# A hybrid attention layer on one core: transposes of keys, queries and augmented rows become float32r products with a float32r identity

## The reference

```python
def dsa_mixer(q, k, v, iq, iw, ik):                       # 8 heads, one shared key/value head
    logits = einsum('bqhd,bsd->bqhs', iqb, ik)             # indexer, 8 heads of 32
    index = einsum('bqh,bqhs->bqs', iwb, relu(logits)) * idx_scale
    _, sel = top_k(index, 256)                            # keys kept for each query
    s = einsum('bqhd,bqkd->bqhk', qb, kg) * scale
    return einsum('bqhk,bqkd->bqhd', masked_softmax(s, valid), vg)

def nsa_mixer(q, k_cmp, v_cmp, k_slc, v_slc, k_win, v_win, gates, ...):   # 8 heads in 2 groups
    kc, vc = compress(k_cmp), compress(v_cmp)             # 127 compressed keys
    # compressed branch, 8 selected blocks of 64 keys, and a window of 512 keys
    return gb[..., 0:1] * o_c + gb[..., 1:2] * o_s + gb[..., 2:3] * o_w
```

## Time and profile before

| | |
|---|---|
| median of three executions | 4019.19 us (4006.82 to 4023.22) |
| the profiled execution, its own time | 4008.02 us |
| its span, first to last instruction | 4006.0 us |
| PE busy over the span | 3669.9 us, 92% |
| DVE, ACT, POOL busy | 46%, 41%, 19% |
| granted clock, mean | 0.945 |

### The profile page before, as it was taken

How to read it: one execution, slowest core, us unless ns; L and a number is a source line. 1 busy time by engine, 2 the same in 40 slices (tenths; PEclk the granted TensorE clock), 3 DMA queues, 4 the chain that set the end, 5 groups by cost and what they waited for, 6 DMA issues and landing times. The chain is left out here.

```text
span 4006.0 us, 56003 instructions
## 1 busy us (share of the span) xinstructions
PE 3669.9 (92%) x19448; PEld 3110.9 (78%) x19448; DVE 1838.5 (46%) x4296; ACT 1650.0 (41%) x2690; POOL 765.1 (19%) x1650
## 2 busy tenths in 40 slices
PE   6999768989898999999999697999999999999997
PEld 5999647877777788888778585788788788878885
DVE  4222145666666666776664343333343243324323
ACT  2000024667666677677765332232232233223321
POOL 0000023454343333332321132000020020002001
PEclk9999768999999999999889898999999999999998
DMA  4221220000000000000000354333333433433342
GB/s 144 74 69 62 67 50 26 24 16 22 16 9 16 15 16 13 10 7 10 4 6 6 124 158 147 105 94 129 103 94 112 135 100 94 142 109 96 94 136 74
DMA packets 302064, 273.15 MB, mean 68 GB/s; under 512 B 32544, under 2 KB 249760, under 8 KB 299680
## 3 DMA queue, kind: packets, MB, share of 16 engines
q1 hardware_dynamic: 300368, 268.31, 21.8%
q10 hardware_dynamic: 1488, 2.20, 0.2%
HBM read 218.57 MB, written 51.90 MB: 68 GB/s over the span
## 5 line engine op out<-in xcount | busy, mean ns | idle before, releaser
L2224 DVE TENSOR_TENSOR f_w_lo<-f_raw,f_w_hi 128x1024 fp32r<-128x1024 f32 x264 | 337.3, 1278 | 883.7 <-ACT f_w_hi L2176 883.7
L2176 ACT ACTIVATE f_w_hi<-f_raw 128x1024 fp32r<-128x1024 f32 x264 | 279.9, 1060 | 882.6 <-PE f_acc L2128 337.2
L1285 ACT ACTIVATE a_p_t<-a_ps_st 128x512 f32<-128x512 f32 x716 | 438.0, 614 | 371.3 <-PE a_ps_st L1175 191.7
L1292 ACT ACTIVATE a_junk_a<-a_index,a_tk 128x384 bf16<-128x384 f32 (+13 forms) x336 | 445.0, 1325 | 110.3 <-DVE a_halves L1402 55.6
L1201 PEld LDWEIGHTS a_ps_o<-a_vsl,a_p_t 128*128 128x128 f32 x2176 | 315.5, 209 | 26.4 <-DVE a_fin L1499 3.4
L2128 PE MATMUL f_gate<-f_x_hi,f_w_hi 128*128 128x512 f32 x704 | 275.1, 391 | 30.2 <-DVE f_w_lo L2224 30.2
L1201 PE MATMUL a_ps_o<-a_vsl,a_p_t 128*128 128x65 f32 x2176 | 298.2, 284 | 2.1 <-DVE a_fin L1499 2.1
L1201 PEld LDWEIGHTS a_ps_o<-a_dv,a_p_t 128*128 128x128 f32 x2176 | 290.0, 194 | 9.0
L2128 PE MATMUL f_acc<-f_w_hi,f_g_hi 128*128 128x512 f32 x704 | 278.6, 396 | 16.4 <-DVE f_y L2280 12.6
L2128 PE MATMUL f_acc<-f_w_lo,f_g_hi 128*128 128x512 f32 x704 | 277.2, 394 | 0.0
L2128 PE MATMUL f_acc<-f_w_hi,f_g_lo 128*128 128x512 f32 x704 | 277.0, 393 | 0.0
(11 more groups left out here) (268 smaller groups left out, 7556.7 us busy)
## 6 DMA issues: line engine op xcount, KB each, us to landing
f_raw<-in_w_gate SPq DMA_DIRECT2D x88, 512.0 KB, 3.8
f_raw<-in_w_up SPq DMA_DIRECT2D x88, 512.0 KB, 3.8
f_raw<-in_w_down SPq DMA_DIRECT2D x88, 512.0 KB, 3.3
z_scratch<-p_z SPq DMA_DIRECT2D x16, 1120.0 KB, 5.2
pw_raw<-in_w_in SPq DMA_DIRECT2D x16, 560.0 KB, 3.8
px_raw<-in_x_t SPq DMA_DIRECT2D x16, 512.0 KB, 6.4
o_scratch<-a_oacc SPq DMA_DIRECT2D x32, 256.0 KB, 2.1
m_o_in<-o_scratch SPq DMA_DIRECT2D x16, 512.0 KB, 4.5
```

What stands on the lines that cost most here:

```text
L1285: act.activation(p_t[:, s % PT_RING, :], ps_st[s % ST_BANKS][:, :], ACT.Exp, scale=SCALE).then_inc(exp_done, 1)
L1292: act.activation(junk_a[:, 0:w], index[t % 2][:, 0:w], ACT.Sign, bias=thr, scale=-1.0, accum_out=cnt).then_inc(counted, 1)
L2176: act.activation(w_hi[:, slot], raw[:, parity], ACT.Copy).then_inc(hi_done, 1)
L2224: dve.tensor_tensor(w_lo[:, slot], raw[:, parity], w_hi[:, slot].bitcast(F32), ALU.subtract).then_inc(lo_done, 1)
```

## The change

Each transposed block becomes an ordinary product of the block, as float32r, with a float32r copy of the identity. The shapes, the operands' roles, the number of TensorE instructions and their order stay: the stationary operand is the block, the moving operand the identity. VectorE makes the copy `ident_r` once, ahead of its other set-up, and TensorE's first transposes wait for that copy instead of for the constants. The augmented rows are declared float32r, so that the three instructions that write them write float32r. The transposes of the compression and mixing stages are not touched.

```diff
+        ident_r = sb("a_ident_r", [P, P], F32R)
...
-        aug_n = sb("a_naug", [P, 2, 8, P])
-        aug_d = sb("a_daug", [P, 8, P])
+        aug_n = sb("a_naug", [P, 2, 8, P], F32R)
+        aug_d = sb("a_daug", [P, 8, P], F32R)
...
-            pool.memset(aug_n[:, :, :, :], 0.0).then_inc(aug_clear, 1)
-            pool.memset(aug_d[:, :, :], 0.0).then_inc(aug_clear, 1)
+            pool.memset(aug_n[:, :, :, :].bitcast(F32), 0.0).then_inc(aug_clear, 1)
+            pool.memset(aug_d[:, :, :].bitcast(F32), 0.0).then_inc(aug_clear, 1)
...
                     src = split[:, b, :] if kind in "KI" else q_hi[:, b].rearrange("p a d -> p (a d)")
-                    mm = pe.transpose(out[:, (b - b0) * P:(b - b0 + 1) * P], src.bitcast(F32), const("ident", 0, P))
+                    mm = pe.matmul(out[:, (b - b0) * P:(b - b0 + 1) * P], src, ident_r[:, :], start=(b == b0), stop=(b == b0 + nb - 1), skip_group_check=True)
                 mm.then_inc(group_turned, 1)
...
-                    mm = pe.transpose(out[:, h * P:(h + 1) * P], aug_of(kind, i)[:, 4 * g + h, :], const("ident", 0, P))
+                    mm = pe.matmul(out[:, h * P:(h + 1) * P], aug_of(kind, i)[:, 4 * g + h, :], ident_r[:, :], start=(h == 0), stop=(h == 3), skip_group_check=True)
                 mm.then_inc(group_turned, 1)
...
-            pe.wait_ge(const_ld, 32)
+            pe.wait_ge(ident_set, 1)
...
             dve.wait_ge(const_ld, 32)
+            dve.tensor_copy(ident_r[:, :], const("ident", 0, P)).then_inc(ident_set, 1)
             mine(dve.tensor_copy(ident_b[:, :], const("ident", 0, P)))
```

More of the change, by code:

```diff
@@ L783, in attention_phase @@
         rows_set = sem("a_rows_set")
+        ident_set = sem("a_ident_set")
         split_done = {k: sem(f"a_split{k}") for k in "KIND"}
```

## The result

The changed kernel takes 4077.36 us, the median of six runs (4065.42 to 4088.94), and the kernel before takes 4013.64 us over its six (4005.95 to 4023.22). The ratio is 1.0157, with a 95% interval of 1.0132 to 1.0181, so the change costs 64 us. The forecast was 4080. The two profiled executions lie a little further apart than the medians, 72 us (4080.2 and 4008.0).

What follows compares the result with a forecast made beforehand. TensorE was taken to bound the attention stage, busy 91% at a mean clock of 0.92. Direct price +10 and clock +54 make +64 us on the profiled 4008.0, or 4072; with the median's offset 4080, range 4030 to 4120.

Steps and rivals of the forecast that it cites:

- TensorE sets the pace and is priced twice, by stream and by clock: Attention stage: TensorE busy 91%; a product costs what it takes from the stream and what it does to the clock.
- The direct price: TensorE's 976 blocks: +0.003 us each and an exposed load behind each of 158 runs, +10 us in all.
- Later rises: Attention stage: blocks stream half as long, so 22 clock rises come later, 154 us more at low clock, 64 us lost.
- The 7 us for each rise: Delay assumed for each of 22 rises, from nine low stretches that ended without transposes, 7.2 us in the mean.
- the one row of 17.0 us: Low stretch from 1919.3 to 1936.3 without a transpose at its end, TensorE busy for 16.65 us; the longest of nine.
- A sixth of it lost in waits: Attention stage: a slower TensorE finds VectorE's maxima ready, so the clock's 64 us become 54 us.
- The number of low stretches about as now: Profile after, attention stage: about as many stretches at clock 0.50 as the 31 before, each longer.
- The start: Start of the attention stage: fourteen transposes alone, clock 1.00 from 533.5; after the change it stays at 0.50 beyond that.
- No clock effect: Rival for the attention stage: the clock does not care, only the direct price counts, +10 us, 4029; chance 0.13.
- A product lifts the clock sooner than a transpose: Rival: 22 low stretches of the attention stage each lose their last 3.4 us, -21 us, 3998; chance 0.06.
- Two products for a block: Rival for TensorE's 976 blocks: each new block is two products, +107 us, about 4126; chance 0.03.
- the 22 stretches: Of 31 low stretches in the attention stage, those with transposes in the last 4 us before the clock rose.

Runs made afterwards that it cites:

- halves: The changed kernel with only the augmented blocks as float32r products, 4037.76 us; with only those of keys and queries, 4026.31 us; the other blocks are transposes.
- the wide blocks: Against the changed kernel, each block except the last of its group moves the identity twice, 256 columns: 4032.64 us, ratio 1.0049 to before.

## Why the prediction was right, step by step

- **TensorE sets the pace and is priced twice, by stream and by clock.** Right. With the other edits alone the time is that of before (1.0009); VectorE, ScalarE and GpSimd have the busy times they had.
- **The direct price, +10 us.** Right in kind: its parts are in the timeline, 0.112 us a block and 0.29 us for the 512-column product behind a run. In size it is 7 us by the estimate over the stage. No run measures it alone, since the clock changes in all of them.
- **Later rises, 154 us more at the low level.** Right in kind and too small: 195 us in the pair of profiles, 175 in the mean of the executions. TensorE's busy share in the added low time was 0.93 and not 0.83, so the gross loss is some 86 to 91 us where I had 64. The 7 us for each rise was the mean of nine stretches of a kernel that still had its transposes. Without them stretches of over 40 us appear (755.8, 1677.4 and 1967.5 in the rows above), with hardly a pause of TensorE in them, where I had bounded a stretch by the one row of 17.0 us. The kernel before has one of 37.6 us too; transposes stood at its end, so it was not among the nine:

```profile
571.00:608.60 37.60, 27.39 (x101) 21.46 (x102) 18.08 (x95) 7.48 (x15) 6.94 (x11) 0.50 0.05 9
```

TensorE paused for a quarter of it.

- **A sixth of it lost in waits, 10 us.** Too small also: 19 us, a fifth of the 89. The two errors went opposite ways, and +64 came out as +64. A part of that is luck: the gross loss was too small by a quarter or more, the forecast for the waits was half of what they took, and in the pair of profiles the stage grew by 70 us, not 64.
- **The number of low stretches about as now.** Wrong: 24 instead of 32. A longer stretch covers what would have been the next one: 571.4 to 629.5 stands where 571.0 to 608.6 and 615.4 to 622.2 stood.
- **The start.** I read the rise at 533.5 behind transposes alone as the sign that they lift the clock. In the changed kernel the same fourteen blocks do not:

```profile
529.60 1.97 PE L1100 MATMUL a_ps_side<-a_ident_r,a_q_hi 128*128 128x128 f32 x8 [8.83 <-DVE a_ident_r L1511]
531.37 1.48 PE L1100 MATMUL a_ps_side<-a_ident_r,a_split 128*128 128x128 f32 x6
535.68 1.97 PE L1100 MATMUL a_ps_side<-a_ident_r,a_q_hi 128*128 128x128 f32 x8 [2.83 <-POOL a_daug L943]
```

```profile
530.10:533.50 3.40, 2.75 (x13) 2.56 (x12) 2.90 (x6) 2.45 (x6) 1.92 (x2) 0.50 0.41 86
533.50:536.90 3.40, 1.22 (x6) 1.22 (x6) 3.06 (x2) 0.48 (x4) 2.05 (x1) 0.50 1.07 210
536.90:564.60 27.70, 20.38 (x74) 16.24 (x73) 7.64 (x26) 8.47 (x18) 7.43 (x18) 0.50 0.36 73
```

The clock stays low until 564.6. This fits, but it is a weaker sign than I took it for. In the kernel with transposes and the other edits, timeline and the window of its first low stretch:

```profile
536.96 1.97 PE L1100 MATMUL a_ps_side<-a_const,a_q_hi 128*128 128x128 f32 x8 [8.85 <-DVE a_ident_r L1511]
538.73 1.49 PE L1100 MATMUL a_ps_side<-a_const,a_split 128*128 128x128 f32 x6
```

```profile
537.00:593.10 56.10, 40.71 (x153) 31.93 (x153) 24.60 (x91) 16.56 (x37) 14.86 (x29) 0.50 0.30 63
```

The same fourteen transposes stand there and the clock stayed low until 593.1. So something besides the transposes decides too, perhaps where such a run falls, and one start proves nothing in either direction. The sums over the stage and the wide blocks carry the conclusion.
- **The rivals.** No clock effect: its sign, a clock of 0.92 in the stage, did not show. A product lifts the clock sooner than a transpose: the page "TensorE: Matmul & The Clock Gate" of the Trainium skill says in Part 4 that transposes don't count as busy in the way products do; here the low time was 253 and 285 us with transposes and 448 with products of the same blocks, so for these float32 transposes the measurement decides against it. Two products for a block: each block is one record, and 0.112 us.
- **Two slips in the sums.** For the case that a product lifts the clock sooner I gave -10 us in one place and -21 as the rival; by its own terms it is -21. And +100 us needs some 12 us for each of the 22 stretches, not 13. Neither moves the forecast.
- **The advice to keep a transpose a transpose** ("Perfetto Trace Analysis", section Transposes, in the Trainium skill) agrees with the result, by 64 us. The muxes that it gives as the reason were not tested.

What stays open: why the whole costs more than its halves. The intervals of the halves' times reach 9 and 5 us each way and that of the whole 10, so the gap of 24 us is not noise alone, but no run tests its cause. Nor does one show what ended a given low stretch; the runs show only that more streaming, wherever it was added, left less low time.

## What to carry to other kernels

Where TensorE bounds a stage and its clock falls after waits, price a cheaper product by what it streams as well as by what it takes: a product that waits for its stationary load costs about the same time and leaves the array without columns for a part of it. Look for products shorter than their stationary load; moving more columns there costs little (6 us here, by the estimate over the stage: 1428.1 against 1422.5), and with the clock it made the kernel faster than either, 3991.66 us against 4011.61 for the kernel before beside it (0.9957). The added columns compute nothing new. Read the clock's share over a whole stage or more than one kernel before drawing on a single rise.

## What the runs showed of the hardware that was not expected

- Float32 PV products of 128 columns in place of 65 cost nearly nothing at the full clock (eight records in 1.05 us instead of 1.00, and the two 512-column products behind them in 0.47 instead of 0.51), and float32r blocks of 256 columns take 0.12 us instead of 0.112.
- The clock can stay at 0.50 for 41.0 us with TensorE busy for 40.84 of them. Being busy is not what lifts it.
- Writing float32r instead of float32 costs GpSimd and VectorE nothing (1277 against 1280 ns, 218 against 218).
- A product that waits for its stationary load slows down with the clock too: 0.21 us a block at the low level against 0.112.
